# Splitting the weights one chunk earlier on ScalarE in a one-core decoder step

## What is computed

```python
xn = rms_norm(x, norm_w)
aq, ak, av, az, mq, mk, mv, mo, mz, ga, gm, mi, mf = split(xn @ w_in)   # 1024 wide each, mi and mf 4
aq, ak = rope(rms_norm(aq)), rope(rms_norm(ak))
attn = causal_attention(aq, ak, av)             # prompt; one MoBA block, so it is plain causal attention
attn_s = moba_sample(aq, ak, av, cache_k, cache_v, page_table)   # samples: best 3 of 4 blocks of 256 cached keys
h, states = mlstm(mq, mk, mv, mi, mf)           # 4 heads of 256, for samples from a stored 256x256 state each
y_att = (attn * silu(az)) @ w_proj_attn
y_ml = (rms_norm(h * sigmoid(mo)) * silu(mz)) @ w_proj_mlstm
y = x + (sigmoid(ga) * y_att + sigmoid(gm) * y_ml) @ w_out
```

## Time and profile before

| | |
|---|---|
| time, median of three runs | 470.21 us (468.83 to 470.4) |
| span of the profiled execution, first to last instruction | 467.2 us |
| the profiled execution's own time | not listed apart; the median of the runs lies 3.0 us above its span |
| TensorE busy (matmuls / weight loads) | 456.2 us (98%) / 413.8 us (89%) |
| VectorE, ScalarE, GpSimd busy | 394.1, 294.4, 100.9 us |
| TensorE's granted clock | full speed throughout |
| DMA | 150.91 MB, mean 323 GB/s |

### The profile page before, as it was taken

How to read it: one execution, slowest core, us unless ns; L and a number is a source line. 1 busy time by engine, 2 the same in 40 slices (tenths; PEclk the granted TensorE clock), 3 DMA queues, 4 the chain that set the end, 5 groups by cost and what they waited for, 6 DMA issues and landing times.

```text
span 467.2 us, 11345 instructions
## 1 busy us (share of the span) xinstructions
PE 456.2 (98%) x3855; PEld 413.8 (89%) x3855; DVE 394.1 (84%) x1610; ACT 294.4 (63%) x490; POOL 100.9 (22%) x181
## 2 busy tenths in 40 slices
PE   6999999999999999999999999999999999999997
PEld 4899899897879888888899889899898898899997
DVE  3898899699999799999899999799999774668861
ACT  4966545686984496995486695666948357324430
POOL 2040421013323213423321332321223110000000
PEclk9999999999999999999999999999999999999999
DMA  8899699749999999999999999998999985457511
GB/s 304 322 353 407 183 322 371 240 158 340 317 416 408 404 368 354 412 410 408 408 380 315 409 412 409 411 372 303 382 415 409 410 334 188 149 180 261 182 48 48
DMA packets 44858, 150.91 MB, mean 323 GB/s; under 512 B 6192, under 2 KB 7796, under 8 KB 44672
## 3 DMA queue, kind: packets, MB, share of 16 engines
q1 hardware_dynamic: 20368, 70.77, 40.8%
q0 software_dynamic: 19008, 67.20, 37.3%
q10 hardware_dynamic: 5424, 12.21, 6.8%
HBM read 137.37 MB, written 12.76 MB: 321 GB/s over the span
## 4 chain that ended last, share of the span: by engine, by line
PE 70%; ACT 10%; DVE 10%; DMA 4%; issue 4%; ACTq 1%; POOLq 0%; SPq 0%; POOL 0%; DVEq 0%
PE pj L534 28%; PE pj L537 13%; PE wk L534 6%; PE pa L717 4%; PE wk L537 3%; DMA kpages<-in_cache_k 3%; DVE kpages L1170 3%; DVE wlo L1071 2%; ACT L838 2%; ACT whi L818 2%; PE wk L487 2%; DVE cslot L1252 2%; PE wk L639 2%; PE wk L673 1%; DMA cst<-in_consts 1%
## 5 line engine op out<-in xcount | busy, mean ns | idle before, releaser
L534 PE MATMUL pj<-xn,whi 128*128 128x264 f32 x1328 | 180.8, 288 | 1.6 <-ACT mqT L976 1.3
L534 PEld LDWEIGHTS pj<-xn,whi 128*128 128x128 f32 x1328 | 168.4, 189 | 10.2 <-issue 6.2
L1071 DVE TENSOR_TENSOR wlo<-wraw,whi 128x1024 fp32r<-128x1024 f32 x112 | 136.1, 1220 | 8.8 <-ACT whi L818 8.3
L818 ACT ACTIVATE whi<-wraw 128x1024 fp32r<-128x1024 f32 x112 | 117.9, 1053 | 23.1 <-PE wk L537 12.9
L1170 DVE CUSTOM_DVE_ANT_0 kpages<-kpages,qbc 128x128 f32<-128x128 f32 x512 | 115.5, 292 | 5.3 <-DMA kpages<-in_cache_k 5.1
L537 PE MATMUL pj<-xn,wlo 128*128 128x264 f32 x664 | 93.8, 284 | 0.4 <-DVE wlo L1071 0.4
L537 PEld LDWEIGHTS pj<-xn,wlo 128*128 128x128 f32 x664 | 85.5, 188 | 0.6 <-DVE wlo L1071 0.6
L404 POOL DMA_DIRECT2D kpages<-in_cache_k x64 | 34.3, 536 | 165.9 <-DVE sco L1170 141.9
L404 POOL DMA_DIRECT2D vpages<-in_cache_v x64 | 33.9, 530 | 57.9 <-issue 38.9
L1170 DVE DVE_READ_ACCUMULATOR2_ANT sco<- 128x1 f32 x512 | 42.8, 84 | 0.0
L717 PE MATMUL pa<-vpages,prob 128*32 128x256 f32 x512 | 34.2, 385 | 1.7 <-ACT prob L876 1.7
(11 more groups left out here) (271 smaller groups left out, 615.0 us busy)
## 6 DMA issues: line engine op xcount, KB each, us to landing
wraw<-in_weights SPq DMA_DIRECT2D x112, 512.0 KB, 6.8
kpages<-in_cache_k POOLq DMA_DIRECT2D x64, 512.0 KB, 8.1
vpages<-in_cache_v POOLq DMA_DIRECT2D x64, 512.0 KB, 10.8
cslot<-in_states SPq DMA_DIRECT2D x16, 512.0 KB, 9.4
out_C_s<-cslot ACTq DMA_DIRECT2D x16, 512.0 KB, 8.1
xres<-in_tokens SPq DMA_DIRECT2D x1, 1056.0 KB, 5.5
out_k_p<-kT ACTq DMA_DIRECT2D x4, 256.0 KB, 10.2
out_v_p<-v_nat ACTq DMA_DIRECT2D x4, 256.0 KB, 4.7
```

The lines of the kernel that those rows point to most:

```text
L534: mm(bank[:, 0:T], whi[:, q, k, :], src[:, g, k, :], start=(k == 0 and g == 0), stop=False)
L818: A(whi[:, n % WSPLIT], wraw[:, n % WRAW], ACT.Copy).then_inc(whi_ready, 1)
L1071: V.tensor_tensor(wlo[:, n % WRAW], wraw[:, n % WRAW], whi[:, n % WSPLIT], ALU.subtract).then_inc(wlo_ready, 1)
```

## The change

The lead becomes four chunks for the high halves and, as LOW follows from it, three for the low halves. With four slots of `whi`, `split_hi(n+4)` waits for chunk n. In the heads the split moves from before the head copy to behind it; at head 0 there are now two splits, one before and one behind the gate activations. The body's list is unchanged but for the chunk numbers. The tail's list is unchanged too: the split stands at the head of each step, before the evacuation. VectorE starts the heads with three low halves and not two.

```diff
-AHEAD = 3
+AHEAD = 4
 LOW = AHEAD - 1
...
                 if h == 0:
                     act.wait_ge(boot, 16)
                     head_copy(h, qT[:, h, :], qkw[:, 0:1], h % 2)
-                    split_hi(h + AHEAD)
+                    split_hi(AHEAD - 1)
                     act.wait_ge(gate_e, 1)
                     ch.link(A(gr[:, 3, :], gr[:, 3, :], ACT.Exp))
                     A(gr[:, 3, :], gr[:, 3, :], ACT.Ln, bias=1.0).then_inc(gate_ln, 1)
+                    split_hi(AHEAD)
                 elif h < HEADS:
-                    split_hi(h + AHEAD)
                     if h >= 2:
 
                         act.wait_ge(norm_ps, h - 1)
                     head_copy(h, qT[:, h, :], qkw[:, 0:1], h % 2)
+                    split_hi(h + AHEAD)
                 if h >= 1:
```

## The result

| | before | after |
|---|---|---|
| time, median | 470.3 us (4 runs, 468.83 to 470.68) | 476.6 us (4 runs, 475.37 to 478.16) |
| span of the profiled execution | 467.2 us | 475.6 us |
| mean granted TensorE clock | 1.000 (profiled execution) | 0.993 in two runs, 0.996 in two |

The ratio is 1.0145, with a 95% interval of 1.0113 to 1.0177. The kernel became slower, as forecast, but by 6.3 us and not by 3.6, and the time lies above the range; two of its four runs, 475.37 and 475.42 us, lie inside it.

The account below looks back on a forecast made before the run. TensorE was taken to bound the kernel, starving for weights only once. Heads 0.95, tail start 2.5, later tail -0.2 and step i = 32 0.3 summed to 3.55 us on 470.21, giving 473.8 us; range 469.8 to 476.2 us.

Parts of the forecast that it names:

- Direction and chain: Whole kernel: slower by 3.55 us, mainly as a late first tail split delays output gate, stores, copy and probability.
- The end of the heads: Chunk 11's split delays inverse root 6, so TensorE gets the last rotated heads later: +0.95 us, bounds 0 and 1.05.
- The body at 0: Rounds: the 0.39 us low-half wait goes, but the probability wait behind it grows as much: 0, gain at most 0.4 us.
- I take 2.5, as the row of the store itself gives it: Start of the tail: second state store issued 2.5 us late, landing 9.4 us after issue, delays TensorE's probability: +2.5 us.
- The upper bound of 4 us: Start of the tail: the cost if the stores also meet the burst of loads that TensorE's stall sets free.
- The scores, -0.2 us: Later in the tail: with TensorE later, its wait of 0.20 us at 372.61 for the last scores goes.
- It holds by 0.3 us, so 0: Tail, i = 13: probability ready at 385.6, TensorE wants it at 385.89; cost 0, at most 0.5 us.
- The last slice: Step i = 32: the merged gates' last slice comes later as its split waits for chunk 103: +0.3 us, bounds 0 and 0.4.
- The drain behind a table load: Tail's second probability: a skill's drain of about 1.38 us would cost a further 1.1 us, giving 474.9; rows speak against it.
- Rival (b): Rounds and heads: the larger lead lets TensorE run through today's waits, 3.4 us gone, 466.8 us; chance 0.06.
- Rival (c): Tail: the store also takes longer, up to 4 us, or the probability at i = 13 comes late: 475.6 us; chance 0.10.

Follow-up runs that it names:

- the wait alone: Kernel before, lead of three, plus one wait: ScalarE waits at tail step i = 0 until chunk 72 is projected; 473.44 us, ratio 1.0098.
- the heads' repair: The change with the heads' split moved behind the inverse root, tail as in the change; 474.14 us, ratio 1.0108.
- the filled wait: The change with 24 extra matmuls, result unused, placed in TensorE's wait for the probability; 474.22 us, ratio 1.0093.
- the shortened chains: Four edits shortening chains TensorE waits for, on the kernel before, both repairs, and five slots with the heads' repair: 469.25, 468.46, 467.18 us.
- both repairs: The change with the heads' split behind the inverse root and the tail's split behind the evacuation in steps 0 to 23; 470.08 us, ratio 1.0012.

## Why the prediction was right or wrong

*Direction and chain: right.* A late first tail split, then the output gate, the stores, the copy, the probability at i = 4: each came in the order the text gives, and the wait alone on the kernel before reproduces it.

*The end of the heads: right.* 0.95 us forecast, 0.76 measured at chunk 9 from the trace's own chunk 0. I held that no later wait would swallow it, and nearly none did: at chunk 43 the heads' repair gives 0.74 us back.

*The body at 0: right*, and shown twice: the low half's wait passed whole into the probability's.

*The stores, "I take 2.5, as the row of the store itself gives it": mis-sized, 3.6 us.* I carried 9.4 us over from the second store's issue, and expected that issue 2.5 us late. It was only 1.3 us late, at 342.03: the store doesn't wait for the evacuation queued ahead of it. But the store landed 12.1 us later. The first store's delay of 3.9 us was the one to carry, as the second lands behind it. The step that failed is the issue time: by the forecast the stores go out 3.4 us apart, near 339.9 and 343.3, and a pair 3.2 us apart in before (268.14 and 271.33) took 7.8 and 9.1 us, so 9.4 fitted. They went out 1.3 us apart, and the second of such a pair took 10.4 to 10.6 us in before already (123.98 and 197.57). The 3.9 us are 3.05 as forecast, 0.5 that TensorE itself was late, and 0.4 between the end of chunk 72 at 336.92 and the split at 337.32, which nothing in the trace explains. The upper bound of 4 us held, but its reason is not what happened: the second store landed at 354.10, before TensorE's stall began at 354.36, so no loads that the stall set free held it up. The Trainium skill ("Trainium Kernel Development and Optimization", Key Constraints) says that DMAs from all issuing engines run on the same 16 DMA engines and interleave. The trace agrees that the path was shared and full: the DMA share was 1.02 to 1.03 from 335 to 355 us.

*The clock: missing from the sum, 2.8 us in the profiled run.* This is the other step that failed, and the one that put the time outside the range: the sum has no term for it. The trace of before had full clock throughout, with no wait of TensorE beyond 0.7 us in the rounds, and I priced a wait of 2.7 us as if nothing followed it. Without it the median would be near 474.2 us, as the filled wait shows, inside the range. No row of before has a slow clock, so its price couldn't be read there; and it differs between executions of one kernel.

*The scores, -0.2 us: open.* The step of -0.47 us at chunk 83 is there in every run but the shortened chains, also with both repairs, where TensorE reaches this place 0.43 us earlier than before. So the wait is missing without TensorE being late; it may be the profiled execution of before alone that had it.

*"It holds by 0.3 us, so 0" at i = 13: wrong, 0.46 us.* I left out the step before. ScalarE's timeline of after:

```profile
386.69 1.06 ACT L818 ACTIVATE whi<-wraw 128x1024 fp32r<-128x1024 f32 x1 [2.79 <-PE pj L537]
...
388.05 1.75 ACTq L888 DMA_DIRECT2D arow<-accr  x2
389.85 0.39 ACT L1058 ACTIVATE sgm<-pj 128x264 f32<-128x264 f32 x1 [1.83 <-PE pj L537]
390.14 1.05 ACT L818 ACTIVATE whi<-wraw 128x1024 fp32r<-128x1024 f32 x1
```

The gather and the two row transfers of i = 12 stand behind the late split too, and their issue holds the queue until 389.80. The evacuation at 389.85 is put down to TensorE, but chunk 84 had long been done.

*The rows at i = 22: not seen, 0.76 us.* The same gather, at i = 21, feeds a transpose one step later. I went through what is queued behind the split at i = 0, 4 and 13, and not at 21.

*The last slice, 0.3 us forecast, 0.63 measured.* The mechanism was right; the excess of 0.3 us is that ScalarE's split began 0.34 us behind VectorE's first product (449.19 and 448.85), though both were released by the same chunk. Why stays open.

*The drain behind a table load:* the rows decide as forecast. In after, load at 356.61 and exponential at 357.90, 1.29 us; and the split before the load ends at 356.58, so no drain of 1.38 us stands ahead of it either.

Rival (b) asked what the larger lead might be worth. It is worth nothing here; with a fifth slot, and once the chains in front of it are shortened, some 2 us (467.18 against 469.25). Rival (c), with a chance of 0.10, comes nearest to what happened: the store took longer, and the probability at i = 13 came late. Its 475.6 us are near the measured time by luck, as it has no term for the clock either.

## What to carry to other kernels

When a prefetch is moved one step earlier with the same number of buffers, its wait moves to the step that frees the buffer: go through every place in every queue where it is issued, and list all that stands behind it until the next wait is met anyway. A lead pays only when the buffer is what TensorE waits for; look for what is late next in either direction, since here shorter chains without the lead and the lead without shorter chains each gave nothing, and together, with a fifth slot, 0.5%. Look in the trace for earlier cases of the very pair whose price you need. And price a stall of some microseconds on TensorE (2.4 were enough here) with what the clock may take after it.

## What the runs showed of the hardware

The clock after a long wait is not certain. With 3.85 us of idle TensorE it fell for 6.8 us; with 3.50 us it held in the profiled run and in one other of the four; with 2.42 us it fell for 3.4 us, and there the fall, at 356.5, came half a microsecond after TensorE had gone back to work at 356.01. So the length of this one wait doesn't settle it, and one kernel gives two clusters of times, 475.4 and 478.0 us in the change.

Two stores issued from ScalarE 1.3 us apart, 512 KB each, landed 3.8 us apart (twice in the kernel before, and in the change) and 4.4 us apart (wait alone). And an issue on that queue ran ahead of activations that still waited: the second store left at 342.03, the evacuation ahead of it in the list ran at 343.76.
